# Side rows of the expert mixer moved from VectorE to ScalarE and GpSimd, token rows for the dot products placed in PSUM

## What is computed

```python
def one_block(xb):                                  # 128 tokens, D = 1024
    q = (xb @ w_q).reshape(P_TOKEN_BLOCK, P_HEADS, 2, P_DKEY // 2)
    s = jnp.einsum('tphd,phnd->tphn', q, subkeys)
    s1, i1 = lax.top_k(s[:, :, 0], P_TOPK)
    s2, i2 = lax.top_k(s[:, :, 1], P_TOPK)
    ...
    eidx = jnp.take_along_axis(cidx, pos, axis=-1)  # 8 x 16 experts of each token
    g = jax.nn.softmax(top, axis=-1)
    act = jax.nn.gelu(jnp.einsum('tped,td->tpe', u[eidx], xb), approximate=False)
    return jnp.einsum('tpe,tped->td', g * act, v[eidx])
```

## Time and profile before

| | us |
|---|---|
| three runs | 2752.54, 2747.76, 2753.51 |
| median | 2752.54 |
| profiled execution, device time | 2751.28 |
| its span, first to last instruction | 2749.5 |

### The profile page before, as it was taken

How to read it: one execution, slowest core, us unless ns; L and a number is a source line. 1 busy time by engine, 2 the same in 40 slices (tenths; PEclk the granted TensorE clock), 3 DMA queues, 4 the chain that set the end, 5 groups by cost and what they waited for, 6 DMA issues and landing times. The chain is left out here.

```text
span 2749.5 us, 22939 instructions
## 1 busy us (share of the span) xinstructions
PE 1960.2 (71%) x6742; PEld 1133.1 (41%) x6742; DVE 1892.7 (69%) x4473; ACT 591.6 (22%) x1595; POOL 863.6 (31%) x772
## 2 busy tenths in 40 slices
PE   7775696597777666776968584778877766766665
PEld 5465364375433223343634262446544422322222
DVE  1326975776777994356698767666787799866665
ACT  2222223232111111123211221322211122211111
POOL 0002322223333341223433423333334333544442
PEclk9788897799888787788989787778988887988888
DMA  9746896699898998899999987657999898999997
GB/s 406 294 159 240 317 364 266 234 357 366 354 368 364 391 382 353 342 367 377 381 420 421 405 315 315 271 225 285 387 390 392 361 387 338 395 390 422 422 421 292
DMA packets 141032, 958.06 MB, mean 348 GB/s; under 512 B 19700, under 2 KB 21748, under 8 KB 25716
## 3 DMA queue, kind: packets, MB, share of 16 engines
q0 software_dynamic: 110592, 805.36, 72.4%
q1 hardware_dynamic: 23024, 147.00, 13.5%
q10 hardware_dynamic: 7300, 4.33, 0.5%
HBM read 953.74 MB, written 2.89 MB: 348 GB/s over the span
## 5 line engine op out<-in xcount | busy, mean ns | idle before, releaser
L667 PE MATMUL acc<-rows,diag 128*128 128x512 f32 x2136 | 1179.9, 705 | 495.9 <-ACT diag L849 480.2
L598 POOL DMA_INDIRECT rows<-in_uv,eidx x768 | 863.4, 1124 | 1847.5 <-PE acc L667 1304.1
L1129 DVE CUSTOM_DVE_ANT_0 rows<-rows,xb 128x1024 f32<-128x1024 f32 x768 | 916.7, 1221 | 277.6 <-DMA rows<-in_uv,eidx 277.2
L667 PEld LDWEIGHTS acc<-rows,diag 128*128 128x128 f32 x2136 | 459.7, 225 | 1139.1 <-ACT diag L849 622.7
L849 ACT ACTIVATE act_out<-act_in 128x2 f32<-128x2 f32 x384 | 78.0, 203 | 1563.2 <-DVE act_in L1129 1558.3
L1118 DVE SCALAR_TENSOR_TENSOR side<-rows,wv,side 128x1024 f32<-128x1024 f32 x234 | 300.6, 1285 | 8.5 <-DVE wv L1113 0.2
L616 PE MATMUL bank<-wt,hT 128*128 128x256 f32 x896 | 201.5, 386 | 8.0 <-ACT hT L849 7.4
L849 ACT ACT_TABLE_LOAD x137 | 175.8, 1283 | 134.6 <-DVE st L1082 33.6
L849 ACT ACTIVATE diag<-small,wv 128x128 f32<-128x128 f32 x534 | 191.9, 387 | 0.1
L616 PEld LDWEIGHTS bank<-wt,hT 128*128 128x128 f32 x896 | 173.6, 194 | 40.9 <-ACT hT L849 9.4
L616 PE MATMUL bank<-hT,wt 128*128 128x256 f32 (+1 forms) x960 | 179.3, 348 | 4.6 <-ACT hT L849 4.6
(11 more groups left out here) (154 smaller groups left out, 1309.2 us busy)
## 6 DMA issues: line engine op xcount, KB each, us to landing
wt<-in_ada_w SPq DMA_DIRECT2D x27, 1024.0 KB
wt<-in_peer_w_q SPq DMA_DIRECT2D x26, 1024.0 KB
rows<-in_ada_w SPq DMA_DIRECT2D x21, 1024.0 KB, 20.8
wt<-in_mlstm_w_in SPq DMA_DIRECT2D x14, 1024.0 KB
rows<-in_uv,eidx POOLq DMA_INDIRECT x768
wt<-in_attn_w_qkv SPq DMA_DIRECT2D x12, 1024.0 KB
rows<-in_mlstm_w_in SPq DMA_DIRECT2D x10, 1024.0 KB, 26.9
wt<-in_attn_w_out SPq DMA_DIRECT2D x8, 1024.0 KB
```

The costliest lines, as they stand in the source:

```text
L598: nc.gpsimd.indirect_dma_start(out=rows[:, r, :], out_offset=None, in_=A["uv"], in_offset=bass.IndirectOffsetOnAxis(ap=eidx[:, b, slot:slo ...
L667: last = nc.tensor.matmul(acc[:, h * 512:(h + 1) * 512], diag[:, r, :], rows[:, r, D + h * 512:D + (h + 1) * 512], start=first and j == 0, ...
L1129: last = V.tensor_tensor_reduce(out=rows[:, r, 0:D], in0=rows[:, r, 0:D], in1=xb[:, place, :], scale=1.0, scalar=0.0, op0=ALU.mult, op1=AL ...
```

## The change

ScalarE scales the side row in place by its weight (`side_scaled`), and GpSimd adds it to `side`, just before it issues the gathers that reuse the ring place. GpSimd also zeroes `side`. The side rows are those of ring places 0, 1, 3 and 4 in every order. ScalarE copies the token rows of an order into a new PSUM tile `xdot` of two banks, and VectorE's dot products read them there instead of in `xb`; the first dots of an order wait for that (`x_placed`), and the copy waits for the last dots of the order before. The steps have four banks instead of six. A step with more than four tiles is no longer put behind the chunk of groups; of those that were, this concerns T2 of the sample (six tiles) and, on VectorE, MOD (eight). In AS all four transposes go first, then the values, and VectorE copies into `prA` itself. TensorE and ScalarE place the choice of the prompt's first quarter after the second query product instead of the third.

```diff
-BANKS = 6
+BANKS = 4
...
-SIDE_PLACES = [(0, 1, 3, 4, 5), (1, 3, 5), (1, 3, 5), (0, 1, 3, 4, 5), (1, 3, 5), (1, 3, 5)]
+SIDE_PLACES = (0, 1, 3, 4)
...
-        if q == 2:
+        if q == 1:
             yield from ((k, 0, "P", 0, 0) for k in ("PT", "PC", "PG"))
...
-        if PLAN[i][0] in late and PLAN[i + 1][0] == "GROUPS":
+        if PLAN[i][0] in late and PLAN[i + 1][0] == "GROUPS" and len(psum_tiles(PLAN[i])) <= BANKS:
...
+        xdot = ctx.enter_context(nc.psum_tensor("xdot", [P, D], F32))
...
+            def add_side(n):
+                ring = n % RING
+                if n % GROUPS == 0:
+                    if n:
+                        pool.wait_ge(sum_read, n // GROUPS)
+                    nc.gpsimd.memset(side[:], 0.0).then_inc(side_zero, 1)
+                    pool.wait_ge(side_zero, n // GROUPS + 1)
+                if not has_side(ring):
+                    return
+                if side_sums(n):
+                    pool.wait_ge(side_summed, side_sums(n))
+                pool.wait_ge(side_scaled, side_sums(n + 1))
+                nc.gpsimd.tensor_tensor(side[:], side[:], rows[:, ring * GS + GS - 1, D:2 * D], ALU.add).then_inc(side_summed, 1)
...
             for n, (l, b) in enumerate(GORDER):
                 for g in range(n * GROUPS, (n + 1) * GROUPS):
+                    if g >= RING:
+                        add_side(g - RING)
...
+            for g in range(len(GORDER) * GROUPS - RING, len(GORDER) * GROUPS):
+                add_side(g)
...
+                    for i in range(4):
+                        t = open_tile(4 + i)
+                        pe.wait_ge(by(i), emptied(i))
+                        transposes(t, [prA[i][:, c * P:(c + 1) * P] for c in range(nk)]).then_inc(tile_full, 1)
                     out = open_tile(8)
                     for i in range(4):
-                        t = open_tile(4 + i)
-                        pe.wait_ge(by(i), emptied(i))
-                        transposes(t, [prA[i][:, c * P:(c + 1) * P] for c in range(nk)]).then_inc(tile_full, 1)
-                        if i:
-                            values(i - 1)
-                    values(3).then_inc(tile_full, 1)
+                        last = values(i)
+                    last.then_inc(tile_full, 1)
...
                 last.then_inc(diags, 1)
+                if has_side(ring):
+                    row = rows[:, ring * GS + GS - 1, D:2 * D]
+                    f(row, row, ACT.Copy, scale=wv[:, ring, GS - 1:GS]).then_inc(side_scaled, 1)
...
+                        if order:
+                            act.wait_ge(dots, order * GROUPS)
+                        f(xdot[:], xb[:, order % 2, :], ACT.Copy).then_inc(x_placed, 1)
...
-                V.scalar_tensor_tensor(side[:], rows[:, ring * GS + GS - 1, D:2 * D], wv[:, ring, GS - 1:GS], side[:],
-                                       ALU.mult, ALU.add).then_inc(side_summed, 1)
...
-                        last = V.tensor_tensor_reduce(out=rows[:, r, 0:D], in0=rows[:, r, 0:D], in1=xb[:, place, :],
+                        last = V.tensor_tensor_reduce(out=rows[:, r, 0:D], in0=rows[:, r, 0:D], in1=xdot[:],
...
+                        dve.wait_ge(x_placed, GORDER.index((s[1], s[2])) + 1)
```

More of the change, by code:

```diff
@@ L844, in _ @@
         def _(act):
-            begin, tile, full, by, emptied, next_of, one, noted = places("A")
+            begin, tile, full, by, emptied, next_of, one, noted, act_tiles = places("A")
             sent = {"stored": 0, "state_out": 0}
@@ L1072, in _ @@
         def _(dve):
-            begin, tile, full, by, emptied, next_of, one, noted = places("D")
+            begin, tile, full, by, emptied, next_of, one, noted, _ = places("D")
             V = nc.vector
```

42 lines of the change are left out of this document (19 added, 23 removed).

## The result

The changed kernel takes 2812.0 us, the median of four runs (2795.3 to 2816.3), beside 2753.0 for the kernel before on the same chip: ratio 1.0194 [1.0137, 1.0251], slower by 53 us (the bare medians differ by 59). Forecast were 2726 us and a range up to 2800; the time lies above it. The kernel before had medians of 2751 to 2758 us on the chips that were used.

The account below looks back on a forecast made before the run. VectorE was taken to lead most chunks, TensorE the image attention. Relief -67, scaling +3, FIN +15, xdot +4, banks +15, first quarter +3 give -27: 2751.3 - 27 + 1.3 = 2726 us, own range 2690 to 2750, overall 2660 to 2800.

Parts of the forecast that it names:

- The relief: Side rows leaving VectorE: 309 us of its time with overheads, taken to shorten the kernel by 67 us.
- ScalarE's latency (+3): Scaling side rows on ScalarE: free but for latency in one chunk in twenty, 3 us.
- xdot (+4): Copying token rows into PSUM for each block: 8 us, half hidden by VectorE's FIN, so 4 us.
- the conversion by the rooms of the blocks: Relief priced by each block's idle DMA time: first 25 us, fourth 12, three others 12, 6 and 12, last 0.
- rival A: VectorE's two-operand SBUF instructions wait for GpSimd's additions: 123 us on `weigh`, half as much elsewhere; centre 2758 us, chance 0.22.
- Four banks, the first quarter, the attention's order, +18 us in all: TensorE's waits for banks cost 15 us, the earlier choice of the first quarter 3, the attention's order 0.
- TensorE's total is the same, 0: In the attention, putting all four transposes ahead of the values was taken to change nothing.
- The additions, 2.2 us and nothing for throughput: Each of 256 GpSimd additions takes 2.2 us, between 1.22 and 3.1, at no throughput cost.
- the limit of 2.9: In a full-rate ring turn, GpSimd isn't the bound with additions of up to 2.9 us each.
- rival B: GpSimd becomes the bound, decided by additions from 2.9 us on; 2799 us at 3.6 us each, chance 0.18.
- the cover named in the prediction: GpSimd waits 1304 us for TensorE, so the ring is full most of the time.
- FIN, +3 us a block: FIN waits for GpSimd's last addition behind two gathers: 3 us each, with a small backlog 15 us in all.

Follow-up runs that it names:

- e3_adds8: The changed kernel with GpSimd's addition on 8 of 1024 columns, every instruction and wait kept: 2667.3 us, ratio 0.9699.
- e1_banks4: The kernel before with all of the change but the side rows' move and xdot: 2738.3 us, ratio 0.9939.
- e7_fin: The changed kernel with the side rows left to TensorE in the last six groups of the first five blocks: 2785.2 us, ratio 1.0096.
- e14_writes_long: The changed kernel with each GpSimd addition replaced by three memsets, the third of 340 columns, which read nothing: 2719.7 us, ratio 0.9860.
- e4_weigh_scalar: The changed kernel with `weigh` as two one-column instructions, the gate a per-partition scalar: 2783.8 us, ratio 1.0099.
- e6_six_banks: The changed kernel with six banks, the late rule and first quarter of before, no xdot, dots reading SBUF only: 2853.6 us, ratio 1.0342.

## Why the prediction was wrong

Step by step, in the order of its sum:

- **The relief, -67 us: right.** With ScalarE's latency (+3) and xdot (+4) it forecast -60; `e3_adds8` against `e1_banks4` gives -66 us, and 76 for 235 us in the kernel before. The sum of the conversion by the rooms of the blocks held; that the gathers' issue falls from 1124 to 959 ns, which it named as possible and took at nothing, is within the 66. The dots at 1.22 us are 1.215, as forecast, and A's sentence on them was right too: left in SBUF they would be 1.42.
- **Four banks, the first quarter, the attention's order, +18 us in all: wrong side.** The runs give -0.0061, -17 us. Banks and quarter cost some 2 us instead of 18. What failed for the attention is "TensorE's total is the same, 0": the instructions are the same, but their time isn't. TensorE closes this loop, as the text had found, and there it is busy 101.1 us instead of 114.6, at a granted clock of 0.82 instead of 0.71.
- **The additions, 2.2 us and nothing for throughput: size nearly right, price wrong.** One takes 2.36 us, beside an estimated 2.25, half of the 4497 ns that the Trainium skill ("GPSIMD Engine Reference", Performance versus the Vector engine) gives for 2048 columns. It is under the limit of 2.9, and rival B's bound isn't reached. But a limit for the steady turn doesn't say that the engine costs nothing below it. GpSimd's wait for TensorE, the cover named in the prediction, shrank from 1304.1 to 712.8 us, and where the ring is empty after a stage a side group costs GpSimd 2.36 + 0.77 + 0.95 + 0.30 + 0.94 = 5.3 us against DMA's 5.0. Memsets of the same length cost 0.0161, 44 us, where 15 stood for FIN alone; some 20 to 25 of them are an estimate for the queue itself, the rest is what memsets hold.
- **FIN, +3 us a block: half of it.** The waits were 7.64, 7.82, 7.67, 6.47 and 6.47 us in the first five blocks and grew by 3.9 to 7.0 us, and `e7_fin` gives 27 us for them. Besides the two gathers and the addition, a second side row is in the backlog: in the last rows of the fifth block GpSimd adds at 2463.21 and again at 2468.55, and FIN starts at 2471.03.
- **Waits on VectorE, 0 in the forecast, rival A: the step that failed.** The forecast priced an addition by GpSimd's throughput and FIN, 15 us in all, and put what it does to VectorE at nothing. Their length costs 136 us (`e3_adds8` against the changed kernel), and VectorE is busy 199 us longer for it. A put 123 us on `weigh` and half as much again elsewhere; the trace shows 152 and 32. It priced them at 27 to 40 us. Their imitation gives 0.0189, 52 us, and additions in place of memsets altogether 0.0334, 92 us. So A had the mechanism and nearly the amount (it had 0.29 of the `weigh` held for 1.1 us each; 104 of 380, 0.27, were, for 1.5 us). Its price was too low: it converted lost time at the mean rate of the relief, 67 for 309, where the imitation cost 0.2 to 0.3 at `weigh` and 0.6 or more at the one-hot products, and it had no term for TensorE's clock. It also gave A without the longer queue. The likeliest case should have been A: the Trainium skill's rule ("SBUF — State Buffer", Who interferes with whom), that a VectorE instruction with two SBUF inputs contends with a reading GpSimd instruction, is what the timeline shows, to the end of the addition. The argument set against it, that gathers don't lengthen `weigh`, was none: a gather's issue on GpSimd isn't an addition. The trace before had a hint the other way: 265 of its gathers were lengthened, up to 2038 ns, most of them beside a dot or a side instruction of VectorE.
- **The blocks.** The first, forecast 25 us shorter, ends 23 us later (756.3 against 733.3); the fourth is 10 longer instead of 10 shorter; the last, "unchanged", is 7 longer. Its loop at the full rate is unchanged indeed (DMA share 1.01); it starts later behind FIN. VectorE's busy time from 230 us to the first FIN is 340 us, not 300, and 308 in the second block, not 273.

Put together from the runs: 2753 - 17 - 66 + 44 + 92 = 2806, which is 1.0194 of 2753. Against the forecast that is -35 us at the attention, banks and quarter, -6 at the relief, +29 at the queue and +92 at the reads: the first three nearly cancel, by luck, and the error of the forecast is what the additions hold. The line between the last two is that of the memsets; with what memsets hold moved over, the 44 and 92 us would be some 20 to 25 and 111 to 116, an estimate.

## What to carry over

Work moved to an engine that reads the same memory isn't free for the engine it leaves: list every small two-operand instruction on the critical engine and estimate its hold as share times half the length of the new neighbour, or give it an operand that isn't held (a PSUM operand for the dots, a per-partition scalar for `weigh`). Then look what comes next on that engine, since the hold can pass to it. An in-order queue that also issues the transfers can charge for added microseconds before its steady limit is reached. A stand-in for a part of the work, like the memsets here, has to be read in the trace like the work itself: they left `weigh` alone, but held copies. And in a loop that one engine closes, look at that engine's clock and not only at its list of instructions: here the attention's order, with the same instructions, was worth 19 us by itself.

## What the runs showed of the hardware

- GpSimd's addition of 128x1024 fp32 takes 2340 to 2830 ns, its copy 1056 in the mean, its memset 966. The two that read hold a VectorE `tensor_tensor` with both inputs in SBUF until they end (`weigh`, mostly 156 ns, took up to 3023 beside additions and up to 1684 beside copies); the memset doesn't hold it (157 in the mean in `e14_writes_long`).
- The memset does hold VectorE's copies, casts and `tensor_scalar` over 32 columns: 1.49, 0.76 and 0.87 us at 2317 to 2320 us of `e14_writes_long`, where such lines take 0.15 to 0.20. Additions hold a copy of two columns too (up to 3.01 us in `e4_weigh_scalar`).
- An instruction of VectorE can be held although it began up to 0.64 us before the addition, while a gather was being issued (13 of 104 in the changed kernel).
- A VectorE `tensor_scalar` of one column whose second input is a per-partition scalar in SBUF isn't held: 195 to 216 ns in 768 instructions beside additions. One of 1024 columns is: 3.11 us at 649.78 us in the changed kernel, where it takes 0.75 without an addition. A custom dot with both inputs in SBUF is lengthened to 1419 ns in the mean, with one of them in PSUM it stays at 1215.
- The first gather behind a GpSimd addition mostly starts 0.76 to 0.80 us after it (213 of 255), one behind another gather 0.30 us after it.
- A gather's issue takes 1088 to 1132 ns in the mean where the dots read both operands from SBUF (1124 before, without additions; 1091 in `e6_six_banks`, with them), and 954 to 966 where they read one from PSUM.
